# A transformer pair on one core: the first slab behind five norms multiplies the unscaled activations, with the shift as a 257th column

## The chip, the cores and the metric

The kernel runs on one NeuronCore of a Trainium2 chip. The metric is the device time of one execution in microseconds (us), the median of the runs shown. All arithmetic is in 32-bit floating point.

## The reference, cut to what matters

Two stacks of two layers each work on x, 256 tokens by 1024 features. The change concerns the first stack alone. Each of its layers has three stages behind a norm (ffn1, the mixer, ffn2):

```python
def modulate(x, gain, shift, scale):
    return rms_norm(x, gain) * (1.0 + scale[:, None]) + shift[:, None]
...
    for l in range(DEPTH):
        mod = cond @ ada_w[l] + ada_b[l]
        sh1, sc1, g1, sh2, sc2, g2, sh3, sc3, g3 = jnp.split(mod, N_MOD, axis=-1)
        h = modulate(x, norm_ffn1[l], sh1, sc1)
        x = x + 0.5 * (1.0 + g1)[:, None] * swiglu(h, ffn1_w1[l], ffn1_w3[l], ffn1_w2[l])
        h = modulate(x, norm_mix[l], sh2, sc2)
        y = token_mix(h, cos, sin, w_in[l], ...)
        x = x + (1.0 + g2)[:, None] * y
        h = modulate(x, norm_ffn2[l], sh3, sc3)
        x = x + 0.5 * (1.0 + g3)[:, None] * swiglu(h, ffn2_w1[l], ffn2_w3[l], ffn2_w2[l])
```

rms_norm divides each token by the root of the mean square of its 1024 features. That root differs by token only; gain times (1 + scale) and the shift differ by feature only. So h @ W is root(token) * ((x * gain) @ W) + shift @ W, and this is what the change makes use of.

## The kernel before

Activations lie feature-major: x, h and sq are 128 partitions by 8 tiles by 256 tokens. TensorE (PE) multiplies weight tiles of 128x128 with 256 moving tokens. The trace holds two matmul records for each such product of 32-bit numbers, so "x16" of a 256-column matmul there is eight products. Weights come as slabs of 16 tiles (1 MB) into a ring of five; SyncE (SP) issues each load once the slab five before it is used, in the order of the code. In some stages it also issues blocks of the modulation matrix ("aring"), which VectorE (DVE) multiplies and sums (ada_sums). Each engine runs its instructions in the order of the code, and counting semaphores join them.

A stage ends with `down` (Strassen-like products of quarters, L587, eleven slabs) or with `linear` (L455). For each pair of feature tiles DVE adds the result into x, and ScalarE (ACT) squares it into sq. Behind the last pair comes the norm: PE sums the squares (`norm`, L610 and L613), ACT takes a logarithm and an exponential (L1020, L1022), DVE refines the root std in four steps (L1323, L1312, L1315, L1317) and writes eight tiles of h (L1333), ACT adds the shift to each (L1026), and PE starts on the next slab with the first tile (L455 in the mixer, L481 in `pairs`, L508 in `quick_pairs`).

`pairs` is the plain up-projection of a swiglu stage: 22 slabs, in each eight products of the gate's weights and eight of the other's. It serves layer 0. `quick_pairs` serves layer 1: slab 0 is plain (L508), slabs 1 to 21 use seven quarter products in place of eight (L527, 28 products of 128 columns), for which GpSimd (POOL) makes two sums of the slab's weights (L410, L411), DVE two more (L1460, L1462) and DVE the sums of tokens of h (L1403 to L1408). The mixer's first job (two output tiles, one slab) holds the raw decay inputs, which ACT moves and processes into `ba` (L1123 on).

There are six norms in the first stack. The one at the very start stays as it is. The five others are called joints here: J1 ffn1 to mixer in layer 0, J2 mixer to ffn2 in layer 0, J3 ffn2 of layer 0 to ffn1 of layer 1, J4 ffn1 to mixer in layer 1, J5 mixer to ffn2 in layer 1.

Of the kernel before, what the change touches and what calls it, by code (L numbers as in the profile page):

```python
# [24 lines left out]
ALU = mybir.AluOpType  # L25
# [4 lines left out]
T = 256  # L30
D = 1024
# [106 lines left out]
def build(nc, wstream, astream, crow, xT, memT, pos, par1, par2, pars, const, outT):  # L138
    ctx = ExitStack()
    with ctx:  # L140
# [63 lines left out]
        gate4 = area(6144, 4, T)  # L204
        down_sums = area(7168, 2, 4, 4, P)
# [64 lines left out]
        RT = 132  # L270

# [124 lines left out]
        @block.gpsimd  # L396
        def _(pool):
            nc.gpsimd.memset(epsc[:], EPS)
            nc.gpsimd.memset(zero8[:], 0.0)
            nc.gpsimd.memset(cbuf[:], 0.0)  # L400
            pool.drain().then_inc(fills_ready, 1)

            def weight_sums(first, s):

                i = first + s
                w = ring[:, i % RING].rearrange("p (a t) -> p a t", a=4)
                new = up_sums[:, s % 2].rearrange("p a u t -> p a (u t)")
# [9 lines left out]
            for s in range(1, NF):  # L417
                weight_sums(quick_up[1], s)
# [3 lines left out]
        def _(pe):  # L422
# [44 lines left out]
            def pairs(rhs, event, after=None):  # L467

                cnt.seen[event] += KD
                for s in range(NF):  # L470
                    slot = at[0] % RING
                    slab_wait(at[0])
                    if s >= 3:
                        pe.wait_ge(bank_free, cnt.value("bank_free", s - 2))
                    elif s == 0:
                        fresh()
                    for n in range(2):
                        for k in range(KD):
                            if s == 0 and n == 0:
# [10 lines left out]
            def quick_pairs(rhs, event):  # L490

                cnt.seen[event] += KD
                rounds = quick_up.index(at[0])
                for s in range(NF):
# [3 lines left out]
                    if s >= 4:  # L498
                        pe.wait_ge(bank_free, cnt.value("bank_free", s - 3))
                    elif s == 0:  # L500
                        fresh()
                    if s == 0:
                        for n in range(2):
                            for m in range(4):
                                for a in range(2):
                                    if n == 0:
                                        pe.wait_ge(sems[event], cnt.value(event, 2 * m + a + 1 - KD))
                                    mm = pe.matmul(psum[:, 0, n * T:(n + 1) * T],  # L508
                                                   lhsT=tile_at(slot, 8 * n + 4 * a + m), rhs=rhs(2 * m + a),
                                                   start=m + a == 0, stop=m == 3 and a == 1)  # L510
                    else:
                        for name, (bk, c) in up_banks.items():
                            if name == "M6":
                                pe.wait_ge(second_sums, 43 * rounds + (3 if s == 1 else 2 * s))
                            if name == "M3":
                                pe.wait_ge(second_sums, 43 * rounds + 2 * s + 1)
# [417 lines left out]
            for layer in range(DEPTH):  # L934
                if layer == 0:
                    norm_all(KD)
                else:
                    norm()
                if layer == 0:
# [4 lines left out]
                norm()  # L944
# [9 lines left out]
                norm()  # L954
                if layer == 0:
                    pairs(lambda k: h[:, k], "operands_of_act")
# [47 lines left out]
        def _(act):  # L1004
# [66 lines left out]
            def swiglu_gate():  # L1071

                for s in range(NF):
# [4 lines left out]
            def quick_swiglu_gate():  # L1078

                act.drain().then_inc(functions_for_dve, 1)  # L1080
                act.wait_ge(slab_used, cnt.next("slab_used"))
                E(gate4[:, 0], psum[:, 0, 0:T], ACT.Silu).then_inc(functions_for_dve, 1)
                for s in range(1, NF):
# [3 lines left out]
                cnt.seen["slab_used"] += NF - 1 + 11  # L1087

            def mixer(layer):
# [5 lines left out]
                def used(j):  # L1095
                    act.wait_ge(slab_used, base + 33 + j + 1)
                    return pair(j % 4)
# [24 lines left out]
                b = used(0)  # L1122
                E(ba[:, 0], b[:, 0], ACT.Identity)  # L1123
                E(ba[:, 1], b[:, 1], ACT.Identity, bias=C("dt")).then_inc(bank_free, 1)
# [6 lines left out]
                E(ba[:, 0], ba[:, 0], ACT.Sigmoid)  # L1131
# [123 lines left out]
            for layer in range(DEPTH):  # L1255
# [13 lines left out]
                swiglu_gate() if layer == 0 else quick_swiglu_gate()  # L1269
# [25 lines left out]
        def _(dve):  # L1295
# [155 lines left out]
            def quick_swiglu(first):  # L1451
# [3 lines left out]
                def second_weight_sums(s):  # L1455
# [3 lines left out]
                    dve.wait_ge(first_sums, 21 * rounds + s)  # L1459
# [7 lines left out]
                for s in range(NF):  # L1467
                    if s == 0:
                        cnt.next("slab_used")
                        dve.wait_ge(functions_for_dve, cnt.next("functions_for_dve"))  # L1470
                        TT(hidden[:, 0], gate4[:, 0], psum[:, 0, T:2 * T], ALU.mult).then_inc(bank_free, 1)
                        second_weight_sums(2)
# [74 lines left out]
            def swiglu(turn):  # L1547
                for s in range(NF):
# [4 lines left out]
                    before_down(s, turn + NF)  # L1553

# [160 lines left out]
            def convolve(layer, c):  # L1715

                n = (8, 0, 16)[c // 4] + 2 * (c % 4)
                if c < 8:
                    dve.wait_ge(bank_free, freed[layer] + 4 + c + 1)
# [290 lines left out]
            for layer in range(DEPTH):  # L2010
                base = layer * SLABS_1
                now[0] = layer
                modulation(layer, 0)
# [4 lines left out]
                if layer == 0:  # L2018
# [6 lines left out]
                down(24, turn=base + 22)  # L2025
                norm(x, KD, lambda k: mulc[:, 8 + k:9 + k], h, squared=True)
                ada_sums(base + 33)
# [12 lines left out]
                residual(KD, 32, turn=base + SLABS_1 - 37)  # L2040
                norm(x, KD, lambda k: mulc[:, 16 + k:17 + k], h, squared=True)
                if layer == 0:
                    swiglu(base + SLABS_1 - 33)
                else:
                    quick_swiglu(base + SLABS_1 - 33)
                if layer == 0:
                    down(40, turn=base + SLABS_1 - 11)
# [315 lines left out]
```

## Time and profile before

| what | value |
|---|---|
| runs | 3047.0, 3049.76, 3047.07 us, median 3047.07 |
| the profiled execution | 3049.54 us, of which the span in the trace is 3047.8 |
| busy share | PE 92%, DVE 51%, ACT 16%, POOL 4% |
| TensorE's mean granted clock | 0.97 of full speed |
| chain that ended last | PE 87%, DVE 7%, ACT 2%, issue 2% |

Times in the trace are counted from the start of the span. In the timeline the bracket behind a row is the engine's idle time before it and what ended that. A row with a count merges neighbouring instructions of one line.

### The profile page before, as it was taken

The numbers are of one execution on the slowest core, as the hardware profiler recorded it, in microseconds if no ns is written. First come the engines' busy times: TensorE is split into PE (matmuls) and PEld (weight loads), VectorE is DVE, ScalarE is ACT, GpSimd is POOL, SyncE is SP. The second block draws the span as 40 slices with busy tenths as digits, with TensorE's granted clock in tenths as the row PEclk, the third lists the DMA queues.
The fourth block names the chain that finished last, engine by engine and source line by source line (L and its number), as shares of the span: only waits on it lengthen the run. The fifth ranks groups of instructions, "written<-read, shape, count | busy, mean of one in ns | idle before, by whom it ended". The sixth has DMA issues, their size and how long they took to land.

```text
span 3047.8 us, 39136 instructions
## 1 busy us (share of the span) xinstructions
PE 2816.1 (92%) x16350; PEld 2525.6 (83%) x16350; DVE 1539.6 (51%) x3018; ACT 478.0 (16%) x827; POOL 108.2 (4%) x92
## 2 busy tenths in 40 slices
PE   4999999979999999999998999999789999988998
PEld 3898878768889899878876799987678898867888
DVE  4466765343446666456535266534325662222565
ACT  1001332231100100241222110002210002111100
POOL 0000000000000140000000033000000000000000
PEclk7999999989999999999998999999899999999999
DMA  7886511312687444331131344442224444322442
GB/s 288 305 300 253 196 67 42 111 69 99 223 305 283 174 167 168 137 111 56 52 129 63 144 141 169 163 154 95 76 96 145 152 167 151 117 105 97 152 152 98
DMA packets 73441, 454.99 MB, mean 149 GB/s; under 512 B 8112, under 2 KB 8880, under 8 KB 27440
## 3 DMA queue, kind: packets, MB, share of 16 engines
q1 hardware_dynamic: 73120, 451.44, 40.8%
q8 instruction: 129, 2.11, 0.3%
q0 software_dynamic: 144, 1.05, 0.1%
q14 instruction: 48, 0.39, 0.0%
HBM read 451.41 MB, written 1.05 MB: 148 GB/s over the span
## 4 chain that ended last, share of the span: by engine, by line
PE 87%; DVE 7%; ACT 2%; issue 2%; DVEq 1%; DMA 1%; ACTq 0%; SPq 0%
PE psum L481 20%; PE psum L455 19%; PE psum L587 13%; PE psum L527 9%; PE psum L726 5%; PE psum L807 4%; PE psum L646 3%; PE psum L670 2%; PE psum L746 2%; PE psum L542 2%; PE psum L658 1%; PE psum L693 1%; PE psum L683 1%; PE psum L508 1%; DVE arena L1315 1%
## 5 line engine op out<-in xcount | busy, mean ns | idle before, releaser
L455 PE MATMUL psum<-h,ring 128*128 128x256 f32 x1840 | 408.7, 385 | 30.1 <-issue 27.6
L455 PEld LDWEIGHTS psum<-h,ring 128*128 128x128 f32 x1840 | 354.9, 193 | 83.7 <-issue 31.2
L481 PE MATMUL psum<-h,ring 128*128 128x256 f32 x1408 | 308.6, 383 | 33.7 <-ACT h L1026 33.7
L481 PEld LDWEIGHTS psum<-h,ring 128*128 128x128 f32 x1408 | 270.6, 192 | 71.6 <-issue 34.4
L481 PE MATMUL psum<-aring,ring 128*128 128x256 f32 x1408 | 304.7, 379 | 1.7 <-issue 1.7
L481 PEld LDWEIGHTS psum<-aring,ring 128*128 128x128 f32 x1408 | 267.6, 190 | 38.4 <-issue 2.4
L587 PE MATMUL psum<-arena 128*128 128x128 f32 x2112 | 249.6, 275 | 0.0
L587 PEld LDWEIGHTS psum<-arena 128*128 128x128 f32 x2112 | 242.6, 192 | 0.0
L726 PE MATMUL psum<-h,ring 128*128 128x256 f32 x1024 | 231.3, 383 | 0.0
L726 PEld LDWEIGHTS psum<-h,ring 128*128 128x128 f32 x1024 | 194.9, 193 | 28.4 <-issue 3.1
L587 PE MATMUL psum<-arena,ring 128*128 128x128 f32 x1584 | 191.6, 275 | 0.0
L587 PEld LDWEIGHTS psum<-arena,ring 128*128 128x128 f32 x1584 | 184.4, 192 | 0.2
L1543 DVE SCALAR_TENSOR_TENSOR aring<-aring,condb 128x1024 f32<-128x1024 f32 x134 | 159.4, 1221 | 18.6 <-DMA aring<-astream 17.0
L455 PE MATMUL psum<-arena,ring 128*128 128x256 f32 x720 | 157.3, 380 | 6.9 <-DVE arena L2037 3.1
L455 PEld LDWEIGHTS psum<-arena,ring 128*128 128x128 f32 x720 | 136.4, 190 | 27.0 <-DVE arena L2037 3.9
L807 PE MATMUL psum<-arena 128*128 128x128 f32 x1088 | 124.7, 276 | 3.6 <-ACT arena L1169 3.6
L807 PEld LDWEIGHTS psum<-arena 128*128 128x128 f32 x1088 | 124.0, 192 | 4.6 <-ACT arena L1169 4.2
L1017 ACT ACTIVATE sq<-x 128x512 f32<-128x512 f32 x48 | 30.3, 631 | 620.4 <-DVEq L1517 382.9
L527 PE MATMUL psum<-arena 128*128 128x128 f32 x1008 | 119.4, 275 | 0.0
L527 PEld LDWEIGHTS psum<-arena 128*128 128x128 f32 x1008 | 115.9, 192 | 0.0
L410 POOL TENSOR_TENSOR arena<-ring 128x512 f32<-128x512 f32 x42 | 54.0, 1286 | 1215.4 <-PEq L594 1018.6
L1418 DVE TENSOR_TENSOR arena<-ring 128x512 f32<-128x512 f32 x66 | 45.6, 691 | 100.6 <-PE psum L587 95.1
(377 smaller groups left out, 3418.7 us busy)
## 6 DMA issues: line engine op xcount, KB each, us to landing
ring<-wstream SPq DMA_DIRECT2D x354, 1024.0 KB, 4.8
aring<-astream SPq DMA_DIRECT2D x134, 512.0 KB, 4.8
ring<-astream SPq DMA_DIRECT2D x10, 512.0 KB, 13.5
kst<-const SPq DMA_DIRECT2D x1, 1344.5 KB, 10.3
x<-xT SPq DMA_DIRECT2D x1, 1024.0 KB, 7.5
arena<-memT POOLq DMA_DIRECT2D x1, 1024.0 KB, 6.7
outT<-h SPq DMA_DIRECT2D x1, 1024.0 KB, 3.9
condb<-crow SPq DMA_DIRECT2D x1, 512.0 KB, 5.5
```

Source lines behind the costliest of these rows:

```text
L410: nc.gpsimd.tensor_tensor(new[:, 0], w[:, 2], w[:, 3], ALU.add)
L455: mm = pe.matmul(out, lhsT=tile_at(at[0] % RING, t), rhs=rhs(k), start=k == 0, stop=k == kt - 1)
L481: mm = pe.matmul(psum[:, s % 4, n * T:(n + 1) * T], lhsT=tile_at(slot, n * KD + k), rhs=rhs(k), start=k == 0, stop=k == KD - 1)
L527: mm = pe.matmul(out, lhsT=w, rhs=v, start=m == 0 and name in ("M1", "M5"), stop=m == 3, skip_group_check=True)
L542: mm = pe.matmul(psum[:, j % 4, t * T:(t + 1) * T], lhsT=lhs(k)[:, t * P:(t + 1) * P], rhs=ring[:, at[0] % RING, k * T:(k + 1) * T], start ...
L587: mm = pe.matmul(out, lhsT=w, rhs=v, start=m == 0 and name in ("M1", "M5", "M3", "M4"), stop=m == NF // 2 - 1, skip_group_check=True)
L646: mm = pe.matmul(psum[:, memory_bank(kind, job), a * T:(a + 1) * T], lhsT=w, rhs=v, start=k == 0, stop=k == KD - 1)
L670: mm = pe.matmul(psum[:, i % 2 * 2 + m, t * T:(t + 1) * T], lhsT=qs[a][:, t * P:(t + 1) * P], rhs=ks[a], start=a == 0, stop=a == len(qs) - 1)
L726: mm = pe.matmul(psum[:, 6 + job % 2, n * T:(n + 1) * T], lhsT=tile_at(i % RING, f % TPS), rhs=h[:, k], start=k == 0, stop=k == KD - 1)
L746: mm = pe.matmul(psum[:, 1 + 2 * (job % 2), n * T:(n + 1) * T], lhsT=tile_at((first + job) % RING, f % TPS), rhs=go[:, k], start=k == 0, s ...
L807: mm = pe.matmul(psum[:, bank + a, u % 4 * P:(u % 4 + 1) * P], lhsT=lhs[:, u], rhs=rhs[:, u], start=True, stop=True)
L1543: STT(out=w, in0=w, scalar=1.0, in1=condb[:], op0=ALU.mult, op1=ALU.mult, accum_out=sums[:, b:b + 1]).then_inc(ada_used, 1)
```

## The change

At the five joints the first slab no longer waits for h. The stage before writes, beside x, the tiles x * gain * (1 + scale) without root and shift into `bare` (128 x 8 x 257); column 257 holds the shift. `first_slab` multiplies all 257 columns, the norm's three products stand after its first six, and DVE's `first_pair` multiplies the output by std. The 257th output column is shift @ W, which is added later as a bias, in ACT's Silu for the gate (`first_gate`), in DVE for the other half (`first_hidden`), and in the mixer on ACT (Identity and Sigmoid with a bias). The norm itself still makes h for all slabs behind the first. In `quick_pairs`, slab 1 becomes the plain one that takes h tile by tile, and the quarter products begin at slab 2; POOL and DVE sum weights from slab 2 on. The modulation of layer 1's first norm moves ahead of the `down` before it.

```diff
+        bare = area(20992, KD, T + 1)
...
-            for s in range(1, NF):
+            for s in range(2, NF):
                 weight_sums(quick_up[0], s)
...
+            def first_slab(v, where):
+
+                slot = at[0] % RING
+                slab_wait(at[0])
+                pe.wait_ge(bank_free, cnt.value("bank_free", -1))
+                for some in ((0, 1, 2, 3, 4, 5), (6, 7)):
+                    for n in range(2):
+                        for k in some:
+                            if n == 0:
+                                pe.wait_ge(operands_of_dve, cnt.next("operands_of_dve"))
+                            mm = pe.matmul(psum[:, 4 + n, 0:T + 1], lhsT=tile_at(slot, where(n, k)), rhs=v[:, k],
+                                           start=k == 0, stop=k == KD - 1)
+                        if n == 0 and some[0] == 0:
+                            norm()
+                mm.then_inc(slab_used, 1)
+                at[0] += 1
...
+                first_slab(bare, lambda n, k: 8 * n + 4 * (k % 2) + k // 2)
...
-                norm()
+                first_slab(bare, lambda n, k: n * KD + k)
                 freed[layer] = cnt.value("bank_free")
-                linear(24, KD, lambda k: h[:, k], event="operands_of_act",
-                       after={11: latent_norms, 13: decay_columns, 19: lambda: head_sums(4)})
+                linear(22, KD, lambda k: h[:, k], event="operands_of_act",
+                       after={9: latent_norms, 11: decay_columns, 17: lambda: head_sums(4)})
...
+            def first_gate():
+
+                act.wait_ge(inputs_for_act, cnt.next("inputs_for_act"))
+                cnt.next("slab_used")
+                E(gate4[:, 0], gate4[:, 0], ACT.Silu, bias=col(FIRST, 0)).then_inc(functions_for_dve, 1)
...
-                second_weight_sums(1)
+                first_pair([gate4[:, 0], hidden[:, 0]]).then_inc(bank_free, 1)
+                D().then_inc(inputs_for_act, 1)
+                second_weight_sums(2)
                 dve.wait_ge(functions_for_dve, cnt.next("functions_for_dve"))
                 token_sums(h, up_tokens, 0, 4).then_inc(second_sums, 1)
...
+            def first_pair(dst):
+
+                dve.wait_ge(slab_used, cnt.next("slab_used"))
+                V.tensor_copy(small[:, FIRST:FIRST + 2], psum[:, 4:6, T])
+                TT(dst[0], psum[:, 4, 0:T], std[:], ALU.mult)
+                return TT(dst[1], psum[:, 5, 0:T], std[:], ALU.mult)
...
+            def unscaled(v, n):
+
+                shift_column(v, n)
+                return dict(scaled_to=v[:, :, 0:T], gain=lambda k: mulc[:, 8 * n + k:8 * n + k + 1])
...
-                down(24, turn=base + 22)
+                down(24, turn=base + 22, **unscaled(bare, 1))
                 norm(x, KD, lambda k: mulc[:, 8 + k:9 + k], h, squared=True)
+                first_pair([ba[:, 0], ba[:, 1]])
...
-                residual(KD, 32, turn=base + SLABS_1 - 37)
+                residual(KD, 32, turn=base + SLABS_1 - 37, **unscaled(bare, 2))
```

How PE's instructions stand at J1, behind the last products of layer 0's first `down`; "arena" with 257 columns is `bare`. Here an order's row counts a product once. Before:

```order
L587 MATMUL psum<-arena 128x128 x16
L587 MATMUL psum<-arena,ring 128x128 x4
L610 MATMUL psum<-sq,kst 128x256
L613 MATMUL psum<-sq,kst 128x256 x2
L455 MATMUL psum<-h,ring 128x256 x96
L758 MATMUL psum<-arena,kst 128x256 x3
```

and now:

```order
L612 MATMUL psum<-arena 128x128 x16
L612 MATMUL psum<-arena,ring 128x128 x4
L479 MATMUL psum<-arena,ring 128x257 x6
L635 MATMUL psum<-sq,kst 128x256
L638 MATMUL psum<-sq,kst 128x256 x2
L479 MATMUL psum<-arena,ring 128x257 x10
L457 MATMUL psum<-h,ring 128x256 x80
L783 MATMUL psum<-arena,kst 128x256 x3
```

Sixteen products on `bare` stand around the norm's three, in the place of the first sixteen on h.

DVE at J3, from the last tile of x to the second pair of weight sums of the quick stage. Before:

```order
L1497 SCALAR_TENSOR_TENSOR x<-arena,mulc,x 128x256
L1560 TENSOR_TENSOR mods<-sums,p 128x16
L1563 SCALAR_TENSOR_TENSOR mulc<-mods,p 128x8
L1323 TENSOR_SCALAR ms<-psum 128x256
...
L1333 SCALAR_TENSOR_TENSOR h<-x,mulc,std 128x256 x8
L1460 TENSOR_TENSOR arena<-arena,ring 128x512
L1462 TENSOR_TENSOR arena<-ring,arena 128x512
L1403 TENSOR_TENSOR arena<-h 128x4x128
...
L1408 TENSOR_TENSOR arena<-arena,h 128x4x128
L1471 TENSOR_TENSOR arena<-arena,psum 128x256
```

and now (L1589 is `first_hidden`):

```order
L1529 SCALAR_TENSOR_TENSOR x<-arena,mulc,x 128x256
L1552 TENSOR_SCALAR arena<-x,mulc 128x256 x2
L1352 TENSOR_SCALAR ms<-psum 128x256
...
L1362 SCALAR_TENSOR_TENSOR h<-x,mulc,std 128x256 x8
L1582 COPY small<-psum 128x2
L1583 TENSOR_TENSOR arena<-psum,std 128x256
L1584 TENSOR_TENSOR arena<-psum,std 128x256
L1489 TENSOR_TENSOR arena<-arena,ring 128x512
L1491 TENSOR_TENSOR arena<-ring,arena 128x512
L1432 TENSOR_TENSOR arena<-h 128x4x128
...
L1437 TENSOR_TENSOR arena<-arena,h 128x4x128
L1589 SCALAR_TENSOR_TENSOR arena<-arena,small 128x256
L1503 TENSOR_TENSOR arena<-arena,psum 128x256
```

The copy and two multiplies of `first_pair` have come between h and the weight sums, and the modulation's two small rows have left.

## Rows read from the trace of the kernel before

**Rows 1.** The page: busy time, share of the span and instructions by engine.

```profile
PE 2816.1 (92%) x16350; PEld 2525.6 (83%) x16350; DVE 1539.6 (51%) x3018; ACT 478.0 (16%) x827; POOL 108.2 (4%) x92
```

**Rows 2.** Waits of PE: us in total, times, longest.

```profile
PE psum L481 <- ACT h L1026: 33.7, 2, 29.9
PE psum L455 <- issue: 27.6, 4, 10.9
```

**Rows 3.** Timeline of J1, from down's last products.

```profile
273.56 0.69 PE L610 MATMUL psum<-sq,kst 128*128 128x256 f32 x2
...
275.11 1.13 PE L613 MATMUL psum<-sq,kst 128*128 128x256 f32 x4 [0.86 <-ACT sq L1017]
...
278.80 3.26 DVE L1333 SCALAR_TENSOR_TENSOR h<-x,mulc,std 128x256 f32<-128x256 f32 x8
...
279.93 10.41 PE L455 MATMUL psum<-h,ring 128*128 128x256 f32 x33 [3.69 <-issue]
```

**Rows 4.** Windows, L610 to first slab's end: length, PE busy (x), PEclk, DMA, GB/s.

```profile
273.56:290.13 16.57, 12.02 (x39) 0.79 0.68 258
789.31:805.88 16.57, 11.58 (x40) 0.79 0.18 68
1019.82:1035.76 15.94, 10.52 (x40) 0.79 0.19 66
1235.97:1250.92 14.95, 10.40 (x39) 0.89 0.20 71
1748.38:1764.99 16.61, 11.62 (x41) 0.79 0.17 64
sum 80.64, PE 56.15; mean PE 11.23
```

**Rows 5.** Windows of four plain slabs and one quick slab (PEclk third from last).

```profile
290.20:317.80 27.60, 27.60 (x129) 24.32 (x128) 5.95 (x13) 5.46 (x11) 0.00 (x0) 1.00 0.30 116
...
1042.16:1048.41 6.25, 6.25 (x58) 6.25 (x57) 3.56 (x9) 0.42 (x1) 2.50 (x2) 1.00 0.43 168
```

**Rows 6.** Timeline: 512-column products; two one-source DVE steps.

```profile
354.72 3.60 PE L658 MATMUL psum<-sq,kst 128*128 128x512 f32 x8
```

```profile
321.14 0.61 DVE L1582 TENSOR_SCALAR arena<-arena,p 128x256 f32<-128x256 f32 x2
```

**Rows 7.** Timeline of J3: POOL's first weight sums beside DVE, then DVE's sums.

```profile
1019.36 0.48 DVE L1497 SCALAR_TENSOR_TENSOR x<-arena,mulc,x 128x256 f32<-128x256 f32 x1
...
1019.91 1.26 POOL L410 TENSOR_TENSOR arena<-ring 128x512 f32<-128x512 f32 x1 [1018.57 <-PEq L594]
1020.15 1.30 DVE L1497 SCALAR_TENSOR_TENSOR x<-arena,mulc,x 128x256 f32<-128x256 f32 x1
1021.13 1.45 POOL L411 TENSOR_TENSOR arena<-ring 128x512 f32<-128x512 f32 x1
...
1029.06 0.68 DVE L1460 TENSOR_TENSOR arena<-arena,ring 128x512 f32<-128x512 f32 x1
...
1032.58 0.69 DVE L1408 TENSOR_TENSOR arena<-arena,h 128x512 f32<-128x512 f32 x1
```

**Rows 8.** Timeline of J5: POOL's sums beside DVE reading PSUM.

```profile
1748.58 0.88 DVE L1381 SCALAR_TENSOR_TENSOR x<-psum,mulc,x 128x256 f32<-128x256 f32 x2 [4.09 <-PE psum L455]
1748.70 1.26 POOL L410 TENSOR_TENSOR arena<-ring 128x512 f32<-128x512 f32 x1 [27.07 <-PE psum L455]
```

**Rows 9.** Timeline, layer 0's first down: end of slab 5's sums, start of slab 6's.

```profile
233.07 0.69 DVE L1423 TENSOR_TENSOR arena<-ring,arena 128x512 f32<-128x512 f32 x1
...
236.04 0.69 DVE L1418 TENSOR_TENSOR arena<-ring 128x512 f32<-128x512 f32 x1 [1.13 <-PE psum L587]
```

**Rows 10.** Timeline of the mixer behind J1: DVE's wait for later slabs.

```profile
311.55 1.49 DVE L1744 TENSOR_TENSOR arena<-arena 128x1280 f32<-128x1280 f32 x1 [22.83 <-ACTq L1134]
```

**Rows 11.** Timeline and window behind a short wait in the mixer.

```profile
470.73 2.08 PE L852 MATMUL psum<-arena 128*128 128x128 f32 x8 [2.54 <-DVEq L1857]
```

```profile
470.70:474.00 3.30, 3.27 (x12) 3.01 (x13) 1.15 (x5) 0.00 (x0) 0.00 (x0) 0.52 0.00 0
```

More of the change, by code:

```diff
@@ L416, in _ @@
             pool.dma_start(memx, memT).then_inc(mem_in, 16)
-            for s in range(1, NF):
+            for s in range(2, NF):
                 weight_sums(quick_up[1], s)
@@ L465, in linear, with pairs @@
                 cnt.seen["bank_free"] += job
-            def pairs(rhs, event, after=None):
+            def first_slab(v, where):
[13 more added lines that the diff above has]
+                at[0] += 1
+            def pairs(rhs, event, after=None, first=None):
+                if first is not None:
+                    first_slab(first, lambda n, k: n * KD + k)
                 cnt.seen[event] += KD
-                for s in range(NF):
+                begin = 0 if first is None else 1
+                for s in range(begin, NF):
                     slot = at[0] % RING
@@ L478, in pairs @@
                         for k in range(KD):
-                            if s == 0 and n == 0:
+                            if s == begin and n == 0:
                                 pe.wait_ge(sems[event], cnt.value(event, k + 1 - KD))
@@ L953, in _ @@
                 linear(8, KD, lambda k: gates[:, 8 + k])
-                norm()
                 if layer == 0:
-                    pairs(lambda k: h[:, k], "operands_of_act")
+                    pairs(lambda k: h[:, k], "operands_of_act", first=bare)
                 else:
@@ L1069, in in_place, with swiglu_gate @@
                 E(dst, dst, func, scale=scale, bias=bias).then_inc(sems[event], 1)
-            def swiglu_gate():
-                for s in range(NF):
+            def first_gate():
+                act.wait_ge(inputs_for_act, cnt.next("inputs_for_act"))
+                cnt.next("slab_used")
+                E(gate4[:, 0], gate4[:, 0], ACT.Silu, bias=col(FIRST, 0)).then_inc(functions_for_dve, 1)
+            def swiglu_gate(first=False):
+                if first:
+                    first_gate()
+                for s in range(1 if first else 0, NF):
                     act.wait_ge(slab_used, cnt.next("slab_used"))
@@ L1080, in quick_swiglu_gate @@
                 act.drain().then_inc(functions_for_dve, 1)
+                first_gate()
                 act.wait_ge(slab_used, cnt.next("slab_used"))
-                E(gate4[:, 0], psum[:, 0, 0:T], ACT.Silu).then_inc(functions_for_dve, 1)
-                for s in range(1, NF):
+                E(gate4[:, 2], psum[:, 2, 0:T], ACT.Silu).then_inc(functions_for_dve, 1)
+                for s in range(2, NF):
                     act.wait_ge(inputs_for_act, cnt.next("inputs_for_act"))
@@ L1120, in move @@
                     moved[0] = filled(point) // TPS
[L1122 to L1124 removed]
+                act.wait_ge(inputs_for_act, cnt.next("inputs_for_act"))
+                E(ba[:, 1], ba[:, 1], ACT.Identity, bias=col(FIRST, 1))
                 act.drain()
@@ L1545, in ada_sums, with first_hidden, swiglu @@
                     blocks[0] += 1
-            def swiglu(turn):
-                for s in range(NF):
+            def first_pair(dst):
[3 more added lines that the diff above has]
+                return TT(dst[1], psum[:, 5, 0:T], std[:], ALU.mult)
+            def first_hidden():
+                dve.wait_ge(functions_for_dve, cnt.next("functions_for_dve"))
+                STT(out=hidden[:, 0], in0=hidden[:, 0], scalar=col(FIRST, 1), in1=gate4[:, 0], op0=ALU.add,
+                    op1=ALU.mult)
+            def swiglu(turn, first=False):
+                if first:
+                    first_pair([gate4[:, 0], hidden[:, 0]]).then_inc(bank_free, 1)
+                    D().then_inc(inputs_for_act, 1)
+                    first_hidden()
+                    ada_sums(turn)
+                for s in range(1 if first else 0, NF):
                     dve.wait_ge(functions_for_dve, cnt.next("functions_for_dve"))
@@ L2012, in _ @@
                 now[0] = layer
-                modulation(layer, 0)
+                if layer == 0:
+                    modulation(0, 0)
                 norm(x, KD, lambda k: mulc[:, k:k + 1], h, squared=True)
@@ L2046, in _ @@
                 if layer == 0:
-                    down(40, turn=base + SLABS_1 - 11)
+                    down(40, turn=base + SLABS_1 - 11, **unscaled(bare, 0))
                 else:
```

52 lines of the change are left out of this document (29 added, 23 removed).

## The prediction

> **What bounds the kernel now.** I read the page first: PE is busy for 2816.1 of 3047.8 us, 92%, and no other engine reaches 60% [rows 1]. The kernel ends when PE has worked through its products, so only time in which PE stands still, or runs slowly, can be won. The list of PE's waits says where it stands. Two of its first entries are waits for h: L481 waited 33.7 us in two instances, of which 29.9 are the very start of the program, and L455 27.6 us in four, in which J1 and J4 lie [rows 2]. No entry there names a DMA.
>
> The timeline of J1 shows what such a wait is made of. PE comes from `down` at 273.56 with the norm's first product, waits 0.86 us for the last squares, and then idles 3.69 us until 279.93 while std and the first tile of h are made [rows 3]. The reader should see the chain in it: from L613's start to h's first DVE step 3.69 us, to PE's start on h 4.82 us, and DVE writes a tile each 0.41 us, a little faster than PE takes one.
>
> The windows add what the waits do not show. From the norm's first product to the end of the first slab the five joints take 16.57, 16.57, 15.94, 14.95 and 16.61 us, 80.64 together, and TensorE's clock averages only 0.79 to 0.89 of 2.4 GHz in them [rows 4]. Elsewhere four plain slabs take 27.60 us at the full clock, 6.90 for each, 0.431 us for each product [rows 5]. At a joint the clock drops to 1.2 GHz behind PE's idle time, and the first slab is the one that pays. A joint holds nineteen products. At full clock and without a gap they are 8.2 us.
>
> **The change part by part.**
>
> *First slab on `bare`.* All its inputs but the last two tiles are there when `down` or the residual ends, since DVE writes them behind each pair of x. PE runs six products (2.6 us), the norm's three, the other ten. The squares that now end 0.86 us late have 2.6 us to come, and so have the two last tiles of `bare`. Length 19 x 0.431 = 8.19. The extra column: four 512-column products take 3.60 us, at most 0.90 each [rows 6], so a column costs (0.90 - 0.431)/256 = 1.8 ns, and sixteen products 0.03 us. That makes 8.22 us a joint, 41.1 for five, and a gain of 80.64 - 41.1 = **39.5 us**.
>
> *Is h ready for the second slab?* L613 now starts 7 x 0.431 = 3.02 us behind the start, h's first tile is usable 4.82 later, at 7.84, and PE asks for it at 8.22. The margin is 0.4 us. PE never idles, and I expect the clock to stay up.
>
> *Slab 1 of the quick stages turns plain.* A quick slab takes 6.25 us [rows 5], a plain one 6.90: 0.65 more, twice. **-1.3 us.** The order of PE's instructions has it: one group of sixteen 256-column products (L533) stays behind the first slab.
>
> *POOL's sums move.* At J3 POOL begins its sums when `down` is done, and DVE's last step on x takes 1.30 us where the one before it took 0.48; POOL's second sum takes 1.45 against 1.26 [rows 7]. That step reads two tiles in SBUF. At J5 POOL's sum begins inside two DVE steps that read PSUM, and they take 0.88 together, 0.44 each: nothing is lost [rows 8]. So the price hangs on what DVE reads. Now POOL's first sums (slab 2) wait for the first slab's end, at 8.3 us, just when DVE is writing the fifth tile of h (first at 3.02 + 3.69 = 6.71, then every 0.41). L1333 reads x and std, both in SBUF, and is nearest to the disturbed row. I take it that each of POOL's two sums holds one step back for its 1.26 us, with one step in between: tiles five and six come at about 10.4 and 11.9 where PE wants them at 9.9 and 10.8, a slip of about 1.5 us in all. Twice: **-3.0 us**. From below it is 0, by [rows 8].
>
> The Trainium skill (SBUF — State Buffer, "Who interferes with whom") says that a DVE instruction with two SBUF inputs and a GpSimd instruction that reads SBUF exclude each other for a whole instruction. The two rows agree with it. By that rule the price of this part is the 3.0 and not the 0, and it is what speaks against the change.
>
> *DVE's new work.* Eight steps of 0.30 us [rows 6] at each joint's stage before, 12 us in all, and a copy and two multiplies (`first_pair`, some 1.1 us) behind h. In the fullest `down`, DVE has finished the sums for slab 5 at 233.76, and slab 5 begins only when slab 4 ends, just before 236.04 [rows 9]; the two steps put ahead of them (0.6 us) fit into that 2.2 us. Without the cover 0.6 us twice in each of the three `down` stages would show, 3.6 us.
>
> Behind the mixers' joints DVE waits 22.83 us for the later slabs [rows 10], which hides `first_pair` and the modulation sums queued behind it. In the quick stages the queue behind `first_pair` is the weight sums and token sums, 1029.06 to 1033.27, 4.2 us [rows 7], of which the second slab's first quarter products with sums are the customer. With POOL's hold DVE leaves h at 12.2, `first_pair` at 13.4, the sums at 17.6; PE needs them behind slab 1 and two of seven products: 8.2 + 1.5 + 6.9 + 1.8 = 18.4. It fits by 0.8. In the plain stage (J2) DVE waits for ACT's Silu, with PE seven microseconds away from needing either.
>
> *SP's queue* keeps its order; nothing that it waits for becomes later than PE's need. PE waits for no slab now, and ring slabs are five ahead. I cost it at nothing; it is rival 2 if not.
>
> **The sum.** 39.5 - 1.3 - 3.0 = 35.2 us. The profiled execution took 3049.54 (span 3047.8) and lies 2.5 above the median of 3047.07. From the median: 3047.07 - 35.2 = **3012 us**, 1.2% faster. Everything behind a joint is released by PE's own products, so I expect the gain to be kept.
>
> **The rivals.**
>
> 1. *PE still stands at the joint.* The margin for h is 0.4 us. Should the chain begin later than I have it (squares behind DVE's new steps, say) by 3 us, PE idles for about 2.6 us. For this the clock is what matters: behind a wait of 2.54 us in the mixer the clock in the next 3.30 us averaged 0.52 [rows 11], so some 1.7 us more go. A joint then gives 4.3 us less, five 21.5: 3034. Against it: ACT is released before the new DVE steps, not behind them. Chance 0.08.
>
> 2. *The gain of layer 0 is lost again.* J1 and J2 lie in stages that carry the modulation blocks; at J1 DMA is busy 0.68 of the window [rows 4]. If loads can't come earlier there, PE will wait for a slab later by what it won, 2 x 8.35 = 16.7 us: 3029. Against it: no wait of PE for a DMA exists. Chance 0.06.
>
> 3. *The odd width costs as 512 columns.* No row has a moving tile above 256 columns on an odd stride of 257. If each of the 80 products took the 0.86 to 0.90 us of [rows 6], that is 0.43 to 0.47 more, 34 to 38 us: no change, 3046 to 3050. Chance 0.03.
>
> 4. *Slower.* The same place, a higher price: the edge is at 35.2 + 6 = 41 us over 80 products, 0.52 us each on top of 0.431. Were the 257th column a product of its own kind, with each product done as two of 512 columns (1.8 us), the loss would be 80 x 1.37 = 110, less the gain: 3122. Nothing in the trace speaks for it but that it isn't shown. Chance 0.02.
>
> **How the numbers follow.** My forecast has 0.81. Its own range is 3004 to 3019: down to 3009 with POOL free, some 4 us less if the windows at 1.2 GHz elsewhere fall luckier (each is 3 to 7 us of half speed, and which waits get one may shift), up by as much, and by 3.6 for DVE's steps. The range reaches to rival 2: **3004 to 3029**. It leaves out rivals 1, 3 and 4, and the tails, some 0.15. This kernel's runs spread over 2.8 us, so that 0.2%, 6 us, is about what can be told from no change. Faster 0.94 (forecast, rivals 1 and 2), same 0.03, slower 0.03.
>
> **What the profile of after would show.** PE from the last product of `down` through the 257-column products and L638 into h without idle time above 0.5 us, joints of 8.2 us, and windows at clock 1.0. L481's successor left with the one wait at the start. At J3 and J5 one or two DVE steps of h with 1.3 us beside POOL's sums, and PE waiting a little over 1 us in L533. The mixers' later waits of PE (for squares, roots) of unchanged length. I am wrong if the 257-column products pitch above 0.44 us, if the clock falls behind the joint all the same, or if new waits for DVE's sums stand at L552 or in `down`.

## The result, and the profile after

The changed kernel takes 3020.30 us (median of four runs, 3016.53 to 3021.86), the kernel before 3048.26 beside it: a ratio of 0.9906, 95% interval 0.9889 to 0.9923. It is faster by 28.0 us (0.9%), where 35 were forecast. The profiled execution has a span of 3019.7 us.

The page and the list of PE's waits, to be held against [rows 1] and [rows 2]. Columns of the waits: us in total, times, longest.

```profile
PE 2810.2 (93%) x16302; PEld 2520.2 (83%) x16302; DVE 1553.8 (51%) x3066; ACT 478.6 (16%) x825; POOL 103.9 (3%) x88
```

```profile
PE psum L503 <- ACT h L1047: 29.9, 1, 29.9
PE psum L457 <- issue: 20.2, 2, 10.9
...
PE psum L533 <- ACT h L1047: 2.0, 3, 0.7
...
PE psum L638 <- ACT sq L1038: 0.8, 1, 0.8
```

Of the waits at L503 for h one is left, at the program's start, and the mixers' two have left L457. The one wait of L638 for squares lies behind the last `down` of stack two. DVE works 14 us more than before, and each `down`, into which most of its new steps go, still takes 68.95 us in both kernels. New is the 2.0 us of L533, the plain slab of the quick stages.

The five joints, as windows from the first product on `bare` to the end of the first slab (length, PE busy, clock, DMA share, GB/s):

```profile
273.58:281.91 8.33, 8.33 (x39) 1.00 0.98 390
782.31:790.57 8.26, 8.26 (x40) 1.00 0.49 168
1004.81:1013.14 8.33, 8.33 (x39) 1.00 0.36 126
1215.70:1224.03 8.33, 8.33 (x39) 1.00 0.36 126
1724.40:1732.65 8.25, 8.25 (x39) 1.00 0.35 128
sum 41.50, PE 41.50; mean PE 8.30
```

41.50 us stand where [rows 4] had 80.64; PE is busy in all of it and the clock is at 2.4 GHz. The timeline of J1 shows the new order; it answers to [rows 3]:

```profile
273.58 2.85 PE L479 MATMUL psum<-arena,ring 128*128 128x257 f32 x12 [0.26 <-issue]
276.27 0.59 PE L635 MATMUL psum<-sq,kst 128*128 128x256 f32 x2
276.70 1.03 PE L638 MATMUL psum<-sq,kst 128*128 128x256 f32 x4
277.56 4.51 PE L479 MATMUL psum<-arena,ring 128*128 128x257 f32 x20
281.91 34.70 PE L457 MATMUL psum<-h,ring 128*128 128x256 f32 x160
```

No row from L635 on has a wait in brackets. Ten products of 257 columns take 281.91 - 277.56 = 4.35 us, 0.435 each against 0.431 for 256.

J3 shows what holds DVE, beside [rows 7]:

```profile
1011.52 5.29 DVE L1362 SCALAR_TENSOR_TENSOR h<-x,mulc,std 128x256 f32<-128x256 f32 x8
...
1013.45 1.27 POOL L412 TENSOR_TENSOR arena<-ring 128x512 f32<-128x512 f32 x1 [1012.11 <-PE psum L479]
1014.69 1.45 POOL L413 TENSOR_TENSOR arena<-ring 128x512 f32<-128x512 f32 x1
1015.04 0.51 ACT L1047 ACTIVATE h<-h,mods 128x256 f32<-128x256 f32 x1 [0.90 <-DVE h L1362]
1016.44 0.91 ACT L1047 ACTIVATE h<-h,mods 128x256 f32<-128x256 f32 x2 [0.90 <-DVE h L1362]
```

The eight steps of h take 5.29 us instead of 3.25; two of them, with one between, take 1.50 and 1.48 us. POOL begins when the first slab ends, and ACT waits 0.90 us twice, once for each of POOL's sums.

**Where the rest of 35 us went.** I cut the span at rows of PE that stand in both kernels. Each stage runs from the end of a `down`, or behind the residual (J2, J5) from the joint's first product, to the first row of the next; the `down` stages themselves are left out, and so are the program's first and last stretch. The joints of the mixers (J1, J4) run to the latent norms' first product (L758, now L783). So J1 before is 273.45 to 324.50, and now 273.33 to 316.44.

| stage | before | again | third | changed | changed again |
|---|---|---|---|---|---|
| J1 | 51.1 | 51.1 | 49.7 | 43.1 | 43.1 |
| rest of mixer 0 | 464.8 | 464.8 | 463.8 | 465.9 | 463.7 |
| J2 and ffn2's up | 161.5 | 161.5 | 161.5 | 153.3 | 153.3 |
| J3 and ffn1's up | 147.2 | 147.2 | 147.2 | 141.9 | 142.0 |
| J4 | 49.4 | 49.4 | 49.4 | 43.1 | 43.1 |
| rest of mixer 1 | 463.1 | 463.1 | 463.1 | 465.8 | 465.9 |
| J5 and ffn2's up | 147.8 | 147.8 | 147.8 | 142.0 | 142.0 |
| st2a, to the middle `down` of stack two | 479.0 | 478.9 | 479.0 | 477.5 | 477.5 |
| st2b, on to the last `down` | 453.0 | 453.0 | 453.0 | 456.0 | 456.0 |

("again" and "third" are later profiles of the same kernels, below.) In the first profiles the stages with a joint give 556.9 - 523.5 = 33.4 us. The stages whose code has not changed give 5.5 back: 1.1, 2.8, -1.4 and 3.0. 33.4 - 5.5 = 27.9, the measured gain. In the changed kernel's second profile they give back only 3.3.

### The profile page after: what moved, and what is told of

It reads as the page before. It is cut to its first block, busy times and chain, and to the rows that moved or that the text cites. A ratio compares the mean times of both kernels' runs of the same rounds, so it can differ in the third digit from the quotient of the medians.

```text
span 3019.7 us, 39078 instructions
## 1 busy us (share of the span) xinstructions
PE 2810.2 (93%) x16302; PEld 2520.2 (83%) x16302; DVE 1553.8 (51%) x3066; ACT 478.6 (16%) x825; POOL 103.9 (3%) x88
## 4 chain that ended last, share of the span: by engine, by line
PE 88%; DVE 7%; ACT 2%; issue 1%; DVEq 1%; DMA 1%; ACTq 0%; SPq 0%
PE psum L503 20%; PE psum L457 19%; PE psum L612 14%; PE psum L552 8%; PE psum L751 5%; PE psum L832 4%; PE psum L671 3%; PE psum L695 2%; PE psum L771 2%; PE psum L567 2%; PE psum L683 1%; PE psum L479 1%; PE psum L718 1%; PE psum L708 1%; DVE arena L1344 1%
## 5 line engine op out<-in xcount | busy, mean ns | idle before, releaser
L457 PE MATMUL psum<-h,ring 128*128 128x256 f32 x1776 | 391.2, 382 | 22.7 <-issue 20.2
L457 PEld LDWEIGHTS psum<-h,ring 128*128 128x128 f32 x1776 | 340.0, 192 | 73.1 <-issue 22.8
L503 PE MATMUL psum<-h,ring 128*128 128x256 f32 x1376 | 298.9, 380 | 29.9 <-ACT h L1047 29.9
L503 PEld LDWEIGHTS psum<-h,ring 128*128 128x128 f32 x1376 | 262.4, 191 | 66.2 <-issue 30.2
L503 PE MATMUL psum<-aring,ring 128*128 128x256 f32 x1408 | 304.7, 379 | 1.7 <-issue 1.7
L503 PEld LDWEIGHTS psum<-aring,ring 128*128 128x128 f32 x1408 | 267.4, 190 | 38.7 <-issue 2.4
L751 PE MATMUL psum<-h,ring 128*128 128x256 f32 x1024 | 233.3, 385 | 0.0
L751 PEld LDWEIGHTS psum<-h,ring 128*128 128x128 f32 x1024 | 196.5, 194 | 28.9 <-issue 2.9
L1575 DVE SCALAR_TENSOR_TENSOR aring<-aring,condb 128x1024 f32<-128x1024 f32 x134 | 159.4, 1219 | 16.6 <-DMA aring<-astream 16.1
L457 PE MATMUL psum<-arena,ring 128*128 128x256 f32 x720 | 157.3, 380 | 6.9 <-DVE arena L2100 3.1
L457 PEld LDWEIGHTS psum<-arena,ring 128*128 128x128 f32 x720 | 136.3, 190 | 27.2 <-DVE arena L2100 3.9
```

The costliest lines, as they stand in the source:

```text
L457: mm = pe.matmul(out, lhsT=tile_at(at[0] % RING, t), rhs=rhs(k), start=k == 0, stop=k == kt - 1)
L503: mm = pe.matmul(psum[:, s % 4, n * T:(n + 1) * T], lhsT=tile_at(slot, n * KD + k), rhs=rhs(k), start=k == 0, stop=k == KD - 1)
L751: mm = pe.matmul(psum[:, 6 + job % 2, n * T:(n + 1) * T], lhsT=tile_at(i % RING, f % TPS), rhs=h[:, k], start=k == 0, stop=k == KD - 1)
L1575: STT(out=w, in0=w, scalar=1.0, in1=condb[:], op0=ALU.mult, op1=ALU.mult, accum_out=sums[:, b:b + 1]).then_inc(ada_used, 1)
```

## The experiments

Times and ratios are against runs of the kernel before on the same chip, whose medians were 3048.53 us for experiments 1 to 4, 3049.21 for 5 to 7 and 3047.59 for 8 and 9. Times of different groups are best compared by their ratios.

**1. The changed kernel again** (no edit).

> The changed kernel once more. Its first profile gained 34.4 us between the five joints' first products and the ends of their first slabs (or slab 1 in the quick stages), and lost about 6 us of it in the mixers and near the end, where its clock stood at 1.2 GHz in other places. Theory A (what the clock does outside the joints differs from one execution to the next): this profile has the same joints within 0.3 us each, and its difference to before in the second mixer and at the end is another one, by 1 us or more. Theory B (the change itself makes the later stages longer, by shifting when DVE and ACT are ready): the second mixer loses 3 to 4 us again, at the same places. Time 3017 to 3022 by both.

Measured: 3021.29 us, 0.9910 (0.9895 to 0.9925). The joints repeat. Mixer 0 took 2.2 us less than in the first profile, but mixer 1 and both stages of stack two repeat to 0.1 us. So theory A, mere chance between executions, is wrong for most of what was lost, though it holds for mixer 0. That mixer 1 loses again (2.8 us, where 3 to 4 were expected) is what theory B forecast. Its cause is the subject of experiments 6 and 9.

**2. Fill the gap of the kernel before with work.**

```diff
                     mm = pe.matmul(psum[:, 7, 0:T], lhsT=ones, rhs=sq[:, k], start=False, stop=k == KD - 1)
                 mm.then_inc(norm_summed, 1)
+                if fillers:
+                    for k in range(8):
+                        pe.matmul(psum[:, 6, 0:T], lhsT=ones, rhs=K("cmask")[:, 0:T], start=k == 0, stop=k == 7)
```

> The kernel before, with eight products of constants (256 columns, 3.45 us) put behind the norm's three at each of the five joints, into a bank that nobody reads; the output is unchanged. It separates the idle time from the clock. Theory A (the joint's cost is an idle part and a slow part, and the clock drops because PE stands idle): h comes at the same time, PE's first slab takes 6.9 us instead of 8.5 to 10, the clock stays at 2.4 GHz, and the kernel gains the slow part of the five joints, 11.8 us less 0 to 2 us: 3036 to 3039. Rival (the first slab is slow for another reason, such as waiting for each tile of h): first slabs stay above 8 us and the time stays within 3 us of before.

Measured: 3043.14 us, 0.9985 (0.9975 to 0.9994). The joints as windows of this kernel:

```profile
274.81:288.33 13.52, 12.42 (x55) 1.00 0.80 289
788.56:802.41 13.85, 12.32 (x56) 1.00 0.23 83
1016.35:1031.90 15.55, 13.86 (x56) 0.89 0.19 69
1232.12:1245.62 13.50, 12.41 (x55) 1.00 0.21 78
1744.37:1758.22 13.85, 12.32 (x57) 1.00 0.21 76
sum 70.27, PE 63.33; mean PE 12.67
```

Against 80.64 the joints lose 10.4 us of length, although not one product less stands in them and h comes no sooner: four keep the clock at 2.4 GHz, and J3, where POOL holds the last step on x and PE stands 1.7 us, does not. The rival is refuted: the first slab of J2 takes 7.1 us (795.27 to 802.41), where it was near 10 before. From [rows 4] to the windows of the changed kernel PE's busy time falls from 56.15 to 41.50 us with as many products, so some 15 of the 39 us were products stretched by the slow clock and 24 were idle time; the fillers win back 10.4 of the 15. The total gain of 5.4 missed the expected 10 to 12; here too the unchanged stages gave back part of what the joints had won, 4.4 us in this profile.

**3. POOL's first sums early.**

```diff
-                pool.wait_ge(slab_used, max(i - 1, first))
+                pool.wait_ge(slab_used, i - 1 if s > 2 else first)
```

> The changed kernel, but POOL's first weight sums in each quick stage wait only for the stage before to be over, not for the first slab. In the changed kernel's profile DVE's eight steps of h took 5.3 us instead of 3.26 in J3 and J5, and PE stood 0.7 and 1.3 us. Theory (the shared access of POOL and DVE is what holds DVE): h takes 3.3 us in both, PE does not stand in slab 1, both quick joints shorten by about 1.3 us; at J3 two steps of DVE on x or bare are held instead, which the 2.6 us of products before the norm hide but for at most 1 us. Total gain over the changed kernel 1.5 to 2.6 us. Rival (DVE is slow there because PE or ACT use the same data): h still takes 5.3 us and nothing is gained.

Measured: 3020.56 us, 0.9906 (0.9889 to 0.9922). J3 in this kernel's timeline:

```profile
1003.95 1.53 POOL L412 TENSOR_TENSOR arena<-ring 128x512 f32<-128x512 f32 x1 [1002.61 <-PEq L619]
1004.65 1.11 DVE L1529 SCALAR_TENSOR_TENSOR x<-arena,mulc,x 128x256 f32<-128x256 f32 x1
1005.44 1.45 POOL L413 TENSOR_TENSOR arena<-ring 128x512 f32<-128x512 f32 x1
...
1005.88 1.42 DVE L1552 TENSOR_SCALAR arena<-x,mulc 128x256 f32<-128x256 f32 x2
...
1010.72 3.26 DVE L1362 SCALAR_TENSOR_TENSOR h<-x,mulc,std 128x256 f32<-128x256 f32 x8
...
1012.34 7.07 PE L533 MATMUL psum<-h,ring 128*128 128x256 f32 x32
```

h takes 3.26 us and PE runs through L533. POOL now holds DVE's step on x (1.11 us) and the two steps on `bare` (1.42, where two alone take 0.61), and nobody waits for either, since six products stand before the norm. From the first product on `bare` to the end of slab 1, J3 takes 15.2 us instead of 16.6, J5 15.2 instead of 17.0. So POOL's shared access is shown as the cause. The forecast 1.5 to 2.6 us don't appear in the median: beside the changed kernel's second profile the joints give 3.2 us, and stack two takes 2.5 more (st2a 480.6, st2b 455.5) and mixer 1 0.7 more.

**4. The norm behind four products.**

```diff
-                for some in ((0, 1, 2, 3, 4, 5), (6, 7)):
+                for some in ((0, 1, 2, 3), (4, 5, 6, 7)):
```

> The changed kernel with the norm's products behind the first four products on bare instead of the first six: h's chain starts 0.86 us earlier. The squares were there 1.5 to 1.9 us behind the joint's start, four products take 1.73. Theory (POOL's sums hold DVE's steps on h from the end of the first slab on): two more tiles of h are out before POOL begins, PE's wait in slab 1 falls from 0.7 and 1.3 us to under 0.5, and the norm waits less than 0.3 us at any joint. Gain 1 to 2 us over the changed kernel. Rival (squares come late): PE waits 0.3 us or more at each of the five, and the gain is lost.

Measured: 3021.04 us, 0.9909 (0.9894 to 0.9923). L533 does not wait, J3 and J5 have the same 15.2 us, and the norm waits for squares nowhere. It is another cure for the same wait, although at J5 one step of h was still held (1.49 us). St2b took 459.4 us, and the median shows nothing.

**5. The norm behind all sixteen.**

```diff
-                        if n == 0 and some[0] == 0:
+                        if n == 1 and some[0] == 6:
                             norm()
```

> The changed kernel with the norm's three products behind all sixteen of the first slab. The algebra, the copies and the number of instructions are as in the changed kernel; only the cover of the chain from the norm to h is taken away. Theory (the gain is that chain, and the slow clock behind it, being covered): PE stands 3.7 us at each joint again, the clock falls to 1.2 GHz behind it, and 3.7 plus 1.5 to 3 us are lost at each of five joints: 26 to 33 us, so that the time is 3041 to 3054, about that of before. Rival (the gain comes from elsewhere, such as earlier waits for the squares or the order of slabs): under 15 us are lost.

Measured: 3045.77 us, 0.9990 (0.9980 to 0.9999). Some 25 us of the changed kernel's gain are gone, a little less than the expected 26 to 33, with all of the algebra in place. (Its ten runs spread from 3042.12 to 3048.45, and the profiled one is the fastest of them.) J2 in PE's timeline, and two windows behind the gaps of J1, where PE starts at 287.24, and J2:

```profile
792.56 1.03 PE L638 MATMUL psum<-sq,kst 128*128 128x256 f32 x4
797.33 3.17 PE L503 MATMUL psum<-h,ring 128*128 128x256 f32 x7 [3.75 <-ACT h L1047]
```

```profile
285.90:290.00 4.10, 2.76 (x13) 1.00 0.01 2
797.30:800.70 3.40, 3.37 (x8) 0.53 0.00 0
```

The gap is back, 3.7 us at J1, J2 and J4, 3.9 at J3 and 4.3 at J5. Behind that of J2 the clock is low, behind that of J1 it stayed up, which is one reason why less was lost: nearly the same idle time costs nothing more or some microseconds more, by where it falls.

In this profile the stages with a joint take 547.5 us together, 24.0 more than in the changed kernel and 9.4 less than before. The 9.4 are not the algebra by itself: the sixteen products now stand ahead of the norm and cover its wait for the last squares, which no joint has here. In the kernel before that wait is

```profile
PE psum L613 <- ACT sq L1017: 6.7, 6, 1.7
```

of which 5.9 us lie in the five joints.

**6. The kernel before, twice more** (no edit).

> The kernel before, once more, for a second profile. Open: the changed kernel's and the filler kernel's joints won 34.4 and 10.4 us, but their medians only 28 and 5.4, and in the last stage (from the down in the middle of stack two to the last down), which is the same code, before's one profile took 453.0 us and the five others 455.5 to 459.4. Theory A (where the clock falls outside the joints is chance, and before's one profile had it cheap): this profile takes 455 or more in that stage, and its joints together differ from 80.6 by 1 us or more. Theory B (something in the change makes the later stages longer): this profile takes 453 again, within 0.5.

> The kernel before, a third profile, for the same question as the second: by theory A the time of the last stage and of the second mixer spread over 2 us or more between the three profiles while the total stays within 5 us; by theory B they repeat.

Measured: 3049.46 and 3048.52 us. Their stages stand in the table above. The second repeats the first to 0.1 us everywhere, the third differs in J1 and mixer 0 alone (its first `down` begins 1.1 us later in the span) and then falls into the same times. So theory A is refuted for the second mixer and for stack two, in three profiles; J1 and mixer 0 do vary, by 1.4 and 1.0 us here. It isn't shown that every execution repeats them: the ordinary runs of the kernel before spread from 3046.0 to 3052.5 us. What was left was why unchanged code takes other times in another kernel. The windows of st2b in before and in the changed kernel:

```profile
2513.00:2965.96 452.96, 421.65 (x1946) 0.98 0.36 128
```

```profile
2481.88:2937.89 456.01, 424.71 (x1946) 0.97 0.35 127
```

The same 1946 records; PE stands idle 31.31 us in the one and 31.30 in the other. The 3.05 us are all in the products' own length, with the mean clock 0.97 instead of 0.98. Inside it, the products behind the squares' wait of the second cross attention (L994, now L1015), before and now:

```profile
2684.21 3.69 PE L994 MATMUL psum<-sq,kst 128*128 128x256 f32 x16 [3.32 <-DVE sq L2165]
```

```profile
2652.79 6.41 PE L1015 MATMUL psum<-sq,kst 128*128 128x256 f32 x16 [3.32 <-DVE sq L2229]
```

The wait is the same 3.32 us, and the same sixteen records take 3.69 us in the one kernel and 6.41 in the other. In the 20 us from their start on PE's mean clock is 0.74 and 0.59.

**7. Both small edits** (3 and 4 together).

> The changed kernel with both small edits, norm behind four products and POOL's first sums early. By themselves each took PE's waits in slab 1 away (16.6 to 15.2 us at J3, 17.0 to 15.2 at J5), so that together they should give no more: 3.2 us over the changed kernel at the joints, 3017 to 3020, with J3 and J5 at 15.2 us each from the first product to the end of slab 1.

Measured: 3017.15 us, 0.9894 (0.9879 to 0.9909). J5 stays at the 15.2 us that either edit gave, J3 takes 15.6: POOL holds DVE's step on x there, and four products no longer cover the squares that come late by it. L638 starts 0.68 us behind L635, where the changed kernel had 0.43. So the two edits get in each other's way a little. The kernel is 3 to 4 us faster than the changed kernel, with intervals that overlap.

**8. Constant products ahead of three waits in each mixer**, on top of 7.

```diff
+            def keep_warm(n):
+
+                for k in range(n):
+                    pe.matmul(psum[:, 5, 0:T], lhsT=ones, rhs=K("cmask")[:, 0:T], start=k == 0, stop=k == n - 1)
...
                     fill(point)
+                    if src:
+                        keep_warm(10)
...
                 fill("rope")
+                keep_warm(13)
...
+                keep_warm(17)
                 pe.wait_ge(operands_of_dve, cnt.next("operands_of_dve"))
                 attention("mla", branch_filler(layer), FILL_BRANCH)
```

> The version with both small edits (norm behind four products, POOL early), and beside it products of constants (256 columns, into a bank that is free there) ahead of three of PE's waits in each mixer: 10 ahead of the wait of 5.2 us, 13 ahead of 6.3, 17 ahead of 8.3, so 4.3, 5.6 and 7.3 us. They add no wait if they are shorter than what PE would have waited. Theory (the slow clock follows PE's idle time, wherever that is): the half-clock windows behind these waits go, some 24 us in each mixer of which most lie beside PE work, and each mixer gains 6 to 10 us: 2998 to 3006. Rival (the products themselves delay the waits' end, or the clock falls for other waits instead): mixers gain under 3 us.

Measured: 3006.14 us, 0.9862 (0.9846 to 0.9879), the fastest of all. PE at the two longest of these waits in mixer 0; L911 are the constants:

```profile
648.40 5.77 PE L911 MATMUL psum<-kst 128*128 128x256 f32 x26
655.56 1.99 PE L950 MATMUL psum<-arena,kst 128*128 128x256 f32 x8 [1.39 <-DVEq L1994]
657.39 0.59 PE L952 MATMUL psum<-arena,kst 128*128 128x256 f32 x2
657.83 7.50 PE L911 MATMUL psum<-kst 128*128 128x256 f32 x34
666.30 1.99 PE L695 MATMUL psum<-arena 128*128 128x256 f32 x8 [0.97 <-DVEq L2010]
```

The waits left are 1.39 and 0.97 us, and behind each of them eight records take 1.99 us. In experiment 7's kernel, without the constants, eight took 3.78 and seven 3.36:

```profile
656.49 3.78 PE L942 MATMUL psum<-arena,kst 128*128 128x256 f32 x8 [6.29 <-DVEq L1985]
669.12 3.36 PE L695 MATMUL psum<-arena 128*128 128x256 f32 x7 [8.31 <-DVEq L2001]
```

The rests of the mixers take 458.0 and 460.7 us instead of 463.5 and 463.4, so 5.4 and 2.7 less. Both miss the expected 6 to 10, and mixer 1 lies where the rival had it. Their mean clocks rise from 0.96 to 0.99 in mixer 0 and to only 0.98 in mixer 1. Against the kernel before on its own chip this kernel gains 41.5 us and experiment 7's 32.1, so the constants come with 9.4 us. The profiles put 8.1 us of it into the mixers and 1.7 into st2a, which has no constants.

**9. Shift stack two by a few products** of constants, on the changed kernel.

```diff
             assert at[0] == DEPTH * SLABS_1, at[0]
+            pe.wait_ge(bank_free, cnt.value("bank_free", -1))
+            for k in range(2):
+                pe.matmul(psum[:, 6, 0:T], lhsT=ones, rhs=K("cmask")[:, 0:T], start=k == 0, stop=k == 1)
```

(four and six in the others)

> The changed kernel with two idle-work products (constants, 256 columns, 0.86 us at full clock, into a bank that nobody reads) ahead of the second stack. By now three profiles of before agree to 0.1 us in most stages and take 453.0 us in the last long stage (stage st2b, from the middle down of stack two to the last down), both profiles of the changed kernel 456.0, though its code there is unchanged. Theory C (which of PE's waits are followed by the slow clock depends on when they fall, so a small shift changes later stages by more or less than itself): st2a and st2b, less the added 0.9 us, differ from 477.5 and 456.0 by 1 us or more in at least one of the three shifted kernels, while PE's waits in them stay the same. Rival B (the change leaves DVE or ACT later in the second stack): shifted kernels have 477.5 and 456.0 in all three.

> As the kernel with two products, but four (1.73 us). Theory C: st2a (less 1.7) and st2b together lie anywhere between 928 and 939, as the unchanged code did in the kernels so far, and the half-clock windows stand behind other waits. Rival B: 933.5 again.

> As the kernel with two products, but six (2.59 us). Theory C and rival B as there: by C the sum of st2a and st2b less 2.6 differs from 933.5 by 1 us or more in at least one of the three, by B in none.

| stage | changed | 2 products | 4 | 6 |
|---|---|---|---|---|
| all up to stack two's shift | same | same within 2.3 | same within 2.3 | same within 0.2 |
| st2a less the products | 477.5 | 480.5 | 479.2 | 478.7 |
| st2b | 456.0 | 455.5 | 459.4 | 453.0 |
| total, one run each | | 3023.72 | 3027.56 | 3022.47 |

The first row's 2.3 is mixer 0, as in experiment 1. The windows of st2b with four and with six products:

```profile
2484.55:2943.93 459.38, 428.07 (x1948) 0.97 0.36 126
```

```profile
2485.92:2938.88 452.96, 421.65 (x1946) 0.98 0.36 128
```

With six products st2b is the 452.96 us of the kernel before to the hundredth, in a kernel that has the whole change; with four it is 6.4 us longer. Idle time is 31.31 us in both, DVE is busy for 175.2 us in both and ACT for 61.0. Rival B is refuted. Two kernels above say the same: experiment 5's, which has the change, took 453.0 us in st2b, and experiment 2's, which has not, 456.2.

## Why the prediction was right, and where it was not

*What bounds it, and what a joint costs:* right. PE's idle time and the slow clock behind it were the cost: of the 39 us at the joints 24 were idle time and some 15 stretched products. Experiment 5 shows that covering the chain from the norm to h is 24.0 of the 33.4 us that the stages with joints gave; the other 9.4 came with the products that cover the wait for squares. By its median that kernel is 3.4 us faster than before.

*First slab on `bare`:* 8.33, 8.26, 8.33, 8.33, 8.25 us against 8.22; 41.5 for 41.1. *The 257th column:* 0.435 us a product against 0.433; rivals 3 and 4 did not come. *The margin for h:* it held where POOL was silent. PE has no wait behind the first slab of J1, J2 and J4.

*POOL's hold:* right in mechanism and size. Forecast was 1.5 us of slip at each quick stage; measured are 2.0 us of recorded waits, 0.7 and 1.3, and about 1.4 and 1.8 us in length (16.6 and 17.0 against 15.2 without it), where I had 3.0 in all. The Trainium skill (SBUF — State Buffer, "Who interferes with whom") had the rule, and experiments 3 and 4 agree with it: moving either side of the collision ends PE's wait. *Slab 1 plain:* J3 and J5 give 5.3 and 5.7 us, all told; forecast were 5.6 and 6.2. The sum over the stages with joints is 33.4 against 35.2.

*DVE's new work* cost nothing in any `down` (68.95 us each, as before), and rivals 1 and 2 did not come.

*The number held with luck.* 3020.3 us is 8 above the forecast of 3012 and 1.3 beyond the forecast's own range of 3004 to 3019. It lies within 3004 to 3029 only because the range was drawn up to rival 2, a wait for slabs, and no such wait stands in the profile. Of the 8 us the joints' stages missed 1.8, stages without a changed line took 5.5, and the kernel before was 1.2 slower beside the new one than in its first runs.

*What failed* is the last step, "everything behind a joint is released by PE's own products, so I expect the gain to be kept". The waits behind the joints did keep their lengths, as I had said (the mixers' two longest, at L695 and L942, are 16.6 and 12.6 us for both mixers together in each of the kernels without constants there). But 5.5 us were lost in the length of the products behind them. I had priced this as luck within the range ("which waits get one may shift"), at 4 us in either direction, and centred the forecast on nothing. It is less a matter of chance than that: from mixer 1 on it repeated in every profile of one kernel, cheaply in the three of before (st2b 453.0) and dearly in both of the changed kernel (456.0). But which of them has it cheap is luck, not a cost of the change, as experiment 9 shows; with another shift the gain would have been some microseconds larger or smaller.

What stays open: which of the waits will be followed by the low clock in a given kernel. I can't tell it from the positions, only that shifts of 0.9 to 2.6 us change it. The shifted kernels were run once each.

## What to carry to other kernels

Where an engine waits for a chain of small steps, look for work behind the wait that needs only part of the chain, and put the chain's own start into the middle of that work: here six products before the norm covered its wait for squares and the ten behind it a gap of 3.7 us, and the same products all before it covered only the first. Where the wait must stay, constant products into a free bank kept TensorE's clock up behind it: three such places in each mixer gave 8.1 us in the mixers. And an edit that moves everything by a few microseconds changes the clock in stages that it doesn't touch: compare idle and busy time of unchanged stages before believing a gain or loss under some 6 us in this kernel.

## What the runs showed of the hardware that I had not expected

- Behind mixer 0, profiles of one kernel agree to 0.1 us in stages of 40 to 480 us, even when one begins 1.1 us later (three of one kernel, two of another); mixer 0 itself varied by 1.0 and 2.2 us; profiles of kernels that differ only in 0.9 to 2.6 us of work ahead of a stage differ by up to 6.4 us in it (453.0 to 459.4), at the same idle time of 31.3 us.
- A gap of 3.7 us was followed by a clock at 1.2 GHz at J2 and by one at 2.4 GHz at J1, in one execution (mean 0.53 and 1.00 in the windows behind), and a wait of 3.32 us by sixteen records in 3.69 us in one kernel and in 6.41 in another.
- POOL's sums hold not only DVE steps with two inputs in SBUF (1.11 us instead of 0.48) but also the two one-source steps from SBUF to SBUF (1.42 instead of 0.61).
